# Redistributing eight levels' filler matmuls in a chunked gated recurrence: 2, 2, 3, 2, 2, 2, 1, 2 in place of two each

## The chip, the cores and the metric

One Trainium2 chip, one of its cores. The engines are TensorE (matrix products, PE in the profile), VectorE (DVE), ScalarE (ACT), GpSimd (POOL) and SyncE (SP, which here only issues transfers). The metric is the device time of the whole kernel in microseconds (us).

## The reference

The program is two residual blocks over 512 tokens of width 1024, in float32. The first block has two layers. In each, one large projection feeds three mixers: a gated recurrence with 8 heads (HGRN2), a latent attention with 8 heads, and a cross attention with 4 heads into a memory of 256 tokens. Their gated outputs are projected back, added and normalised. The second block has two feed-forward parts, a neighbourhood attention with a pooling branch, and a last gated part. The change touches only the recurrence:

```python
def _chunk_gated_recurrence(q, k, v, logf):
    """S_t = diag(f_t) S_{t-1} + k_t v_t^T ; o_t = S_t^T q_t, chunkwise."""
...
        decay = jnp.exp(jnp.minimum(diff, 0.0)) * tri[:, :, None]
        A = jnp.einsum('bhtsd,bhsd->bhts', qc[:, :, :, None, :] * decay, kc)
        o = (jnp.einsum('bhts,bhsv->bhtv', A, vc)
             + jnp.einsum('bhtd,bhdv->bhtv', qc * jnp.exp(b), state))
```

## The kernel before

The recurrence is computed in two groups of four heads per layer. A chunk is 128 tokens. Within a chunk the decayed scores are built in levels, doubling the distance that they span: level 0 is the diagonal, level 7 joins the two halves of 64. At level n, TensorE multiplies K blocks by Q blocks (L1094; 128 instructions at levels 0 to 5, 64 at levels 6 and 7) for four heads, into PSUM banks 4 to 7. VectorE then, in its phase of level n + 1, works in two pairs of heads: it takes the products of level n out of PSUM under a mask (L1923, from level 2 on), then multiplies a decay factor into Q (L1941), into K (L1942) and into the running factors (L1943). TensorE's level n waits for VectorE's pair 0 before head 0 and for pair 1 before head 2. So a level has two halves, and its second half is what can wait longer.

TensorE would be idle while VectorE works, so the function `beside` hands each level a number of pieces of a projection, which run behind the four heads' products. A projection of 1024 rows is a Block: two units of weights of 512 rows, four output banks (0 to 3), so eight pieces, each one unit on one bank. The order of pieces is fixed. In the first group it is: seven pieces of the values, eight of the gate, eight of the next group's queries. I write them by unit and bank: value pieces 01, 02, 03, 10, 11, 12, 13, gate pieces 00 to 13, query pieces 00 to 13. With two each, level 2 is followed by value pieces 11 and 12, level 3 by value piece 13 and gate piece 00, level 5 by gate pieces 03 and 10, level 6 by gate pieces 11 and 12.

A projection is computed in three passes (L902, L903, L904) from a high and a low part of each operand. For each tile of raw weights, loaded by SyncE (L832), ScalarE makes the high part (L1255) and GpSimd subtracts it from the raw tile to make the low part (L851). ScalarE does this two units ahead, and a unit's buffer is free only when TensorE has finished the unit three before it. So when a unit's last piece ends, the casts that waited for it follow at once, up to four, and GpSimd's subtractions behind them.

Finished banks are taken out by VectorE (values: a copy, L1631) or by ScalarE (gate: SiLU, L1276). VectorE reads them with a delay. It keeps a list of pending pieces: in each level, after the multiplications of pair 0, it takes pieces off until two are left, after those of pair 1 until one is left, and then adds the level's own pieces to the list.

After the levels come the turning of K (L1105), the states (L1112) and the read-out (L1118, L1120), each behind pieces of its own. The second group of a layer has its own call of `beside` with other blocks.

Of the kernel before, what the change touches and what calls it, by code (L numbers as in the profile page):

```python
# [121 lines left out]
def beside(blocks, *shares, first_pieces=()):  # L122


    pieces = list(first_pieces) + [pc for b in blocks for pc in b.pieces()]
    assert len(pieces) == sum(n for _, n in shares), (len(pieces), sum(n for _, n in shares))
    for ph, n in shares:
        first = 1 if len(ph.slots) > 1 and ph.kind != "level" else 0
        room = len(ph.slots) - first
        for i in range(n):  # L130
            ph.slots[first + i * room // n].append(pieces.pop(0))
# [171 lines left out]
def build(nc, x, x_t, mem_t, positions, w_in, w_uq, w_uk, w_uv, w_mk, w_mv, w_out, ln_g, ln_b, cols_in,  # L303
# [3 lines left out]
    with ctx:  # L307
# [47 lines left out]
        def col(name, i=0):  # L355
            return cols[:, COLS[name][0] + i:COLS[name][0] + i + 1]
# [68 lines left out]
        def transpose(src, tiles, dest, gain, src_fn=None):  # L425
            add(Phase("transpose", pe=tiles, act=tiles, dve=tiles, writes=dest, src=src, tiles=tiles,
                      dest=dest, gain=gain))
# [6 lines left out]
        def out_blocks(l, group):  # L434
            return [Block(w_cols(w_out[l], group * 512, 4, n * 512, 512), 4, 512, "nat", "z" if group == 3 else "y",
                          "residual_sum" if group == 3 else "residual", "dve", (n, group == 0)) for n in range(2)]
# [41 lines left out]
        for l in range(DEPTH):  # L478
            W = w_in[l]

            def blk(off, width, kind, evac, engine, arg, late=False):
                return Block(w_cols(W, 0, KD, off, width), KD, width, kind, "x", evac, engine, arg, late=late)
# [6 lines left out]
            for g in range(2):  # L489
                add(blk(HG_OFF[1] + 512 * g, 512, "tr", "forget", "act", None))  # L490
                add(Phase("forget", dve=1, layer=l, group=g))
                values = blk(HG_OFF[2] + 512 * g, 512, "nat", "copy", "dve", V)
                if g == 0:
                    add(queries[0])
                    add(Phase("between"))
                    plan[-1].slots[0] = values.pieces()[:1]
                else:
                    add(values)
                levels = [Phase("level", pe=4 if level <= LEVELS else 0, act=int(level in (3, LEVELS + 1)),
                                dve=0 if level == 0 else 4 + (level == LEVELS + 1), level=level, slots=2,  # L500
                                free_running=level > 0) for level in range(LEVELS + 2)]
                turn, states = Phase("key_turn", pe=3, act=3), Phase("states", pe=3, dve=3)
                read, gated = Phase("read_out", pe=4, act=4, dve=4), Phase("hg_norm", act=1, dve=1)
                gate = blk(HG_OFF[3] + 512 * g, 512, "nat", "silu", "act", G)
                ahead = latent if g else queries[1]
                if g == 0:

                    beside([gate, ahead], *((ph, 2) for ph in levels[:8]), (turn, 2), (states, 1), (read, 1), (gated, 3),
                           first_pieces=values.pieces()[1:])
                else:  # L510
                    beside([gate] + out_blocks(l, 0) + [ahead], *((ph, 2) for ph in levels[:8]), (turn, 2),
                           (states, 1), (read, 1), (gated, 4))
                for ph in levels:

                    ph.together = True
                for ph in levels + [turn, states, read, gated]:
                    add(ph)
                add(Late(ahead))
                transpose(G, 4, "y", col("hg_gain", l))
# [3 lines left out]
            gate = blk(MLA_GATE_OFF, 512, "tr", "silu", "act", G)  # L523
# [73 lines left out]
        def blk2(off, kind, evac, engine, arg, width=512, late=False):  # L597
            return Block(w_cols(w_in2, 0, KD, off, width), KD, width, kind, "x", evac, engine, arg,
                         banks=4 if kind == "nat" else width // P, late=late)
# [9 lines left out]
        gate, rest = blk2(2048, "nat", "sigmoid", "act", SG2), Phase("between")  # L609
# [1603 lines left out]
```

How the kernel before makes its waits and increments, by code:

```python
        def wait(eng, semaphore, value):  # L757
            if value > 0:
                eng.wait_ge(semaphore, value)
# [1 line left out]
        def units_over(eng, n):  # L761
            if n > 0:
                eng.wait_ge(*unit_end[n - 1])
# [46 lines left out]
        @block.sync  # L811
# [14 lines left out]
                if u == 10:  # L826
                    sp.dma_start(xs[:, :, :], x.rearrange("(t p) n -> p t n", p=P)).then_inc(x_loaded, 16)
                if u >= 2:
                    wait(sp, low_done, low_upto[u - 1][0])
                    wait(sp, low_done_dve, low_upto[u - 1][1])
                sp.dma_start(raw[:, u % 2, 0:nk, 0:b.width], b.w[:, k0:k0 + nk, :]).then_inc(raw_loaded[u % 2], 16)
            for t in range(T):
                for n in range(2):
                    sp.wait_ge(dve_step, finish.dve + 2 + 2 * t + n)
                    cut = slice(n * 512, (n + 1) * 512)
                    sp.dma_start(out[t * P:(t + 1) * P, cut], xs[:, t, cut]).then_inc(stored, 16)
            sp.wait_ge(stored, 16 * 2 * T)
# [2 lines left out]
        @block.gpsimd  # L842
        def _(pool):
            for u, (b, k0, nk) in enumerate(units):
                for k in range(nk):
                    if low_on_dve(u, k):
                        continue
                    pool.wait_ge(high_done, tiles_upto[u] + k + 1)
                    s = (slice(None), u % 3, k, slice(0, b.width))
                    pool.tensor_tensor(wl[s], raw[:, u % 2, k, 0:b.width], wh[s].bitcast(F32),
                                       ALU.subtract).then_inc(low_done, 1)
```

## Time and profile before

| | us |
|---|---|
| median of 3 runs | 2115.13 (2115.03 to 2115.35) |
| the profiled execution | 2115.07 |
| its span | 2113.3 |
| TensorE busy | 2089.2 (99%) |
| TensorE waiting for VectorE at the levels (L1094) | 2.6, in 2 waits |

The page gives each engine's busy time and its share of the span, and the span in 40 slices of about 53 us. The first groups of the two layers lie at 104 to 184 us and at 584 to 663 us. The view of stretches gives busy times between two times that are chosen, here the starts of two levels in sequence, so the length of a stretch is one level, its pieces and any wait.

### The profile page before, as it was taken

To read this page: it belongs to the slowest core of one execution; us is meant where nothing else is said; L and a number is where in the kernel's file an instruction comes from. 1 tells how busy PE (TensorE), PEld (TensorE's weight loads), DVE (VectorE), ACT (ScalarE), POOL (GpSimd) and SP (SyncE) were. 2 spreads that over 40 slices of the span, in tenths; PEclk is the share of its full clock that TensorE was granted. 3 is DMA by queue.
4 is the path that set the end of the run, shared out by engine and by line. 5 is a ranking of instruction groups with operands and counts; after the bars stand their busy time and mean duration, and the time that the engine had idled before them with its cause. 6 is when DMAs were issued, how large, how long until landed. Compare 5 with 4: busy or idle time off the path is not lost.

```text
span 2113.3 us, 33496 instructions
## 1 busy us (share of the span) xinstructions
PE 2089.2 (99%) x13820; PEld 1741.6 (82%) x13820; DVE 894.8 (42%) x1653; ACT 789.8 (37%) x1611; POOL 868.0 (41%) x680
## 2 busy tenths in 40 slices
PE   8999999999999999999999999999999999999998
PEld 7878888778978888778888888888888888888886
DVE  6173565535373465526432211433422612222264
ACT  5424335554423325455422222345433432222244
POOL 4633433232543433233354444343444345454423
PEclk9999999999999999999999999999999999999999
DMA  7522223122222223122242332242233133332222
GB/s 247 178 65 80 78 67 100 41 80 80 80 82 80 77 68 100 41 81 70 76 144 83 118 98 83 89 135 80 66 114 100 61 110 101 109 108 92 100 70 90
DMA packets 98679, 196.65 MB, mean 93 GB/s; under 512 B 3680, under 2 KB 12256, under 8 KB 98144
## 3 DMA queue, kind: packets, MB, share of 16 engines
q1 hardware_dynamic: 95072, 183.25, 26.6%
q10 hardware_dynamic: 3456, 11.27, 1.5%
q8 instruction: 109, 1.79, 0.3%
q14 instruction: 42, 0.34, 0.1%
HBM read 192.41 MB, written 2.10 MB: 92 GB/s over the span
## 4 chain that ended last, share of the span: by engine, by line
PE 59%; ACT 1%; DVE 0%; issue 0%; DVEq 0%
PE ps L902 18%; PE ps L903 18%; PE ps L904 18%; PE ps L1017 1%; PE ps L1157 1%; PE ps L1025 0%; PE ps L1034 0%; PE ps L1180 0%; PE ps L1200 0%; PE ps L1189 0%; PE ps L1070 0%; PE ps L1052 0%; ACT L1581 0%; PE ps L974 0%; PE ps L1210 0%; PE ps L1062 0%
## 5 line engine op out<-in xcount | busy, mean ns | idle before, releaser
L851 POOL TENSOR_TENSOR wl<-raw,wh 128x512 fp32r<-128x512 f32 (+2 forms) x676 | 867.8, 1307 | 1220.6 <-ACT wh L1255 1210.8
L1255 ACT CAST wh<-raw 128x512 fp32r<-128x512 f32 (+2 forms) x692 | 380.7, 604 | 773.3 <-PE ps L904 672.8
L902 PE MATMUL ps<-xh,wh 128*128 128x512 f32 (+1 forms) x1376 | 514.2, 374 | 1.2 <-issue 1.2
L904 PE MATMUL ps<-xh,wl 128*128 128x512 f32 (+1 forms) x1376 | 509.1, 370 | 0.0
L903 PE MATMUL ps<-xl,wh 128*128 128x512 f32 (+1 forms) x1376 | 508.7, 370 | 0.0
L902 PEld LDWEIGHTS ps<-xh,wh 128*128 128x128 f32 x1376 | 259.4, 189 | 46.1 <-issue 3.9
L904 PEld LDWEIGHTS ps<-xh,wl 128*128 128x128 f32 x1376 | 259.1, 188 | 44.6
L903 PEld LDWEIGHTS ps<-xl,wh 128*128 128x128 f32 x1376 | 259.4, 188 | 42.1
L902 PE MATMUL ps<-wh,xh 128*128 128x512 f32 (+1 forms) x608 | 239.1, 393 | 0.2 <-issue 0.2
L904 PE MATMUL ps<-wh,xl 128*128 128x512 f32 (+1 forms) x608 | 234.4, 386 | 0.0
L903 PE MATMUL ps<-wl,xh 128*128 128x512 f32 (+1 forms) x608 | 234.4, 385 | 0.0
L902 PE MATMUL ps<-wh,yh 128*128 128x512 f32 x496 | 198.0, 399 | 0.2
L904 PE MATMUL ps<-wh,yl 128*128 128x512 f32 x496 | 193.6, 390 | 0.0
L903 PE MATMUL ps<-wl,yh 128*128 128x512 f32 x496 | 193.4, 390 | 0.0
L1651 DVE TENSOR_TENSOR work<-ps,work 128x512 f32<-128x512 f32 x44 | 30.3, 688 | 383.3 <-PE ps L904 383.3
L902 PEld LDWEIGHTS ps<-wh,xh 128*128 128x128 f32 x608 | 114.2, 188 | 22.6 <-issue 1.4
L904 PEld LDWEIGHTS ps<-wh,xl 128*128 128x128 f32 x608 | 114.2, 188 | 21.8
L903 PEld LDWEIGHTS ps<-wl,xh 128*128 128x128 f32 x608 | 114.3, 188 | 20.4 <-issue 0.2
L902 PEld LDWEIGHTS ps<-wh,yh 128*128 128x128 f32 x496 | 93.3, 188 | 20.5 <-POOL wl L851 0.8
L904 PEld LDWEIGHTS ps<-wh,yl 128*128 128x128 f32 x496 | 93.1, 188 | 19.9
L903 PEld LDWEIGHTS ps<-wl,yh 128*128 128x128 f32 x496 | 93.3, 188 | 18.5
L1647 DVE TENSOR_TENSOR side<-side,ps 128x512 f32<-128x512 f32 x88 | 59.3, 686 | 106.0 <-PE ps L904 103.4
(273 smaller groups left out, 2436.2 us busy)
## 6 DMA issues: line engine op xcount, KB each, us to landing
raw<-w_in SPq DMA_DIRECT2D x58, 1024.0 KB, 5.2
raw<-w_out SPq DMA_DIRECT2D x20, 1024.0 KB, 5.0
raw<-f1g SPq DMA_DIRECT2D x10, 1024.0 KB, 5.1
raw<-f1u SPq DMA_DIRECT2D x10, 1024.0 KB, 5.1
raw<-f1d SPq DMA_DIRECT2D x10, 1024.0 KB, 5.0
raw<-f2g SPq DMA_DIRECT2D x10, 1024.0 KB, 5.2
raw<-f2u SPq DMA_DIRECT2D x10, 1024.0 KB, 5.1
raw<-f2d SPq DMA_DIRECT2D x10, 1024.0 KB, 5.1
```

The lines of the kernel that those rows point to most:

```text
L851: pool.tensor_tensor(wl[s], raw[:, u % 2, k, 0:b.width], wh[s].bitcast(F32), ALU.subtract).then_inc(low_done, 1)
L902: pe.matmul(o, still[0], move[0], start=k0 + k == 0, stop=False)
L903: pe.matmul(o, still[0], move[1], start=False, stop=False)
L904: mm = pe.matmul(o, still[1], move[0], start=False, stop=k0 + k == b.ktiles - 1)
L1017: mm = pe.matmul(ps[:, 4 + h, 0:width], q_heads[:, 2 * p + h, cut], k_heads[:, p, h, 0:width], start=True, stop=True)
L1157: mm = pe.transpose(ps[:, 4 + 2 * (t % 2) + b, f * P:(f + 1) * P], src[:, t, (4 * b + f) * P:(4 * b + f + 1) * P], ident[:, :])
L1255: act.copy(wh[:, v % 3, k, 0:width], raw[:, v % 2, k, 0:width]).then_inc(high_done, 1)
L1647: ins = dve.tensor_copy(dst, src) if first else dve.tensor_tensor(dst, dst, src, ALU.add)
L1651: link(dve.tensor_tensor(tmp, src, SG[:, j, :], ALU.mult))
```

## The change

The eight levels of the first group get 2, 2, 3, 2, 2, 2, 1 and 2 pieces. The total is 16 as before, and the order of the pieces is unchanged. A level with three pieces runs all three behind its four heads. Level 2 is now followed by value pieces 11, 12 and 13, level 3 by gate pieces 00 and 01, level 4 by 02 and 03, level 5 by 10 and 11, level 6 by 12 alone; level 7 keeps gate piece 13 and query piece 00.

```diff
                 if g == 0:
 
-                    beside([gate, ahead], *((ph, 2) for ph in levels[:8]), (turn, 2), (states, 1), (read, 1), (gated, 3),
+                    beside([gate, ahead], *((ph, n) for ph, n in zip(levels, (2, 2, 3, 2, 2, 2, 1, 2))), (turn, 2),
+                           (states, 1), (read, 1), (gated, 3),
                            first_pieces=values.pieces()[1:])
```

## Rows read from the trace of the kernel before

**Rows 1.** The page: engines' busy time; TensorE by slices.

```profile
PE 2089.2 (99%) x13820; PEld 1741.6 (82%) x13820; DVE 894.8 (42%) x1653; ACT 789.8 (37%) x1611; POOL 868.0 (41%) x680
PE   8999999999999999999999999999999999999998
```

**Rows 2.** Waits of TensorE, whole span: us in total, times, longest.

```profile
PE ps L1094 <- DVE work L1943: 2.6, 2, 1.3
```

**Rows 3.** Stretches, layer 0, levels 3, 4 and 6: length, engines' busy time (instructions), clock, DMA.

```profile
125.98:134.37 8.39, 7.09 (x154) 5.71 (x153) 8.18 (x15) 2.19 (x4) 1.86 (x2) 1.00 0.26 98
134.37:141.28 6.91, 6.91 (x154) 5.65 (x153) 6.58 (x10) 0.00 (x0) 4.11 (x3) 1.00 0.23 59
148.19:154.99 6.80, 6.80 (x89) 5.52 (x88) 4.43 (x8) 3.49 (x5) 2.58 (x2) 1.00 0.01 2
```

**Rows 4.** Stretches, layer 1, level 3.

```profile
605.50:613.90 8.40, 7.09 (x154) 5.71 (x153) 8.19 (x15) 2.19 (x4) 1.86 (x2) 1.00 0.27 102
```

**Rows 5.** Timeline of TensorE, level 3's second half, pieces, level 7: start, length.

```profile
128.02 0.73 PE L1094 MATMUL ps<-work 128*32 128x16 f32 x64 [1.30 <-DVE work L1943]
128.68 0.50 PE L902 MATMUL ps<-wh,xh 128*128 128x512 f32 x1
...
135.62 0.50 PE L902 MATMUL ps<-wh,xh 128*128 128x512 f32 x1
...
154.99 1.98 PE L1094 MATMUL ps<-work 128*32 128x64 f32 x64
```

**Rows 6.** Timeline of VectorE, its levels 3 to 5.

```profile
120.66 1.73 DVE L1941 TENSOR_TENSOR work<-work 128x512 f32<-128x512 f32 x1
122.32 1.77 DVE L1942 TENSOR_TENSOR work<-work 128x512 f32<-128x512 f32 x1
...
124.67 0.68 DVE L1631 COPY work<-ps 128x512 f32<-128x512 f32 x1
125.27 0.72 DVE L1923 COPY_PREDICATED work<-level_mask,ps 128x256 f32<-128x256 uint8 x1
...
127.35 0.61 DVE L1943 TENSOR_TENSOR work<-work 128x256 f32<-128x256 f32 x1
...
128.48 0.42 DVE L1923 COPY_PREDICATED work<-level_mask,ps 128x256 f32<-128x256 uint8 x1
...
130.26 0.44 DVE L1943 TENSOR_TENSOR work<-work 128x128 f32<-128x128 f32 x1
...
133.01 1.38 DVE L1943 TENSOR_TENSOR work<-work 128x128 f32<-128x128 f32 x1
...
135.18 0.43 DVE L1923 COPY_PREDICATED work<-level_mask,ps 128x256 f32<-128x256 uint8 x1 [0.19 <-PE ps L1094]
```

**Rows 7.** Timeline of VectorE, its level 7.

```profile
148.94 0.44 DVE L1923 COPY_PREDICATED work<-level_mask,ps 128x256 f32<-128x256 uint8 x1 [2.91 <-PE ps L1094]
149.41 0.69 DVE L1941 TENSOR_TENSOR work<-work 128x512 f32<-128x512 f32 x1
...
151.32 1.36 DVE L1941 TENSOR_TENSOR work<-work 128x512 f32<-128x512 f32 x1
...
153.32 0.19 DVE L1943 TENSOR_TENSOR work<-work 128x16 f32<-128x16 f32 x1
```

**Rows 8.** Timeline of GpSimd, the second burst and a single subtraction.

```profile
132.51 5.97 POOL L851 TENSOR_TENSOR wl<-raw,wh 128x512 fp32r<-128x512 f32 x4 [8.96 <-ACT wh L1255]
...
150.84 1.29 POOL L851 TENSOR_TENSOR wl<-raw,wh 128x512 fp32r<-128x512 f32 x1 [3.22 <-ACT wh L1255]
```

**Rows 9.** Timeline of ScalarE, casts of the second burst and the first SiLUs.

```profile
131.81 2.19 ACT L1255 CAST wh<-raw 128x512 fp32r<-128x512 f32 x4 [11.92 <-PE ps L904]
...
148.37 1.28 ACT L1276 ACT_TABLE_LOAD   x1 [2.11 <-PE ps L904]
149.66 0.60 ACT L1276 ACTIVATE work<-ps 128x512 f32<-128x512 f32 x1
...
152.38 0.60 ACT L1276 ACTIVATE work<-ps 128x512 f32<-128x512 f32 x1 [1.61 <-PE ps L904]
```

## The prediction

> **What bounds the kernel now.** I read the page first: TensorE is busy 99% of the span, and its row of slices shows nines from the second slice on [rows 1]. So a change can only count if it alters TensorE's work or its waits. The waits of TensorE come next [rows 2]: the matmuls of the recurrence's levels (L1094) waited for VectorE twice, 2.6 us in all, the only wait of the changed code. The table of stretches, one per level, shows where [rows 3, 4]: from one level's first matmul to the next it is 6.91 us for a level with two pieces, but 8.39 us after level 3 in layer 0 and 8.40 us after level 3 in layer 1. The chip spends 1.48 and 1.49 us there, 2.97 us in all. TensorE's rows show how it comes about [rows 5]: level 3 starts at 125.98 [rows 3] with heads 0 and 1, and its second half, heads 2 and 3, starts only at 128.02, 0.06 us after VectorE's L1943 (start 127.35, 0.61 long [rows 6]) ends. Level 3's second half needs what VectorE makes of level 2's second pair of heads.
>
> **What is removed.** A piece is 12 matmuls. Two SiLUs of ScalarE that follow pieces on their banks start 2.72 us apart (149.66 and 152.38) [rows 9], so a piece is 2.72 us of TensorE. With three pieces behind level 2, level 3 starts at 125.98 + 2.72 = 128.70. A level's half is 0.63 us (134.37 to the first piece behind it at 135.62 is 1.25 [rows 3, 5]), so its second half is due at 129.33. VectorE is a little later than before: level 3 of its program now finds four pieces pending and not three, so two bank copies (L1631) stand between its pairs of heads. One costs 0.60 (124.67 to 125.27 [rows 6]). Its pair ends at 127.96 + 0.60 = 128.56, 0.77 before it is needed. The wait goes: -1.48 us a layer.
>
> The total of pieces is 23 before and after, in the same order, with the same switches between levels and pieces. That costs nothing by itself. No DMA, matmul or copy is added. SyncE's loads follow GpSimd's subtractions and so move with them by up to 3 us; in the stretches concerned the DMA share is 0.01 to 0.26 and TensorE waits for no load [rows 3], so I cost that at nothing (uncovered, it would show as a wait of L902 for GpSimd). Bank reuse is free too: the first gate piece needs the copy that VectorE makes at 125.35, and starts near 130.
>
> **What is late next: level 4.** Here I think most of the gain goes. Moving a piece forward moves the end of its weight unit, and with it a burst of four high parts on ScalarE and four low parts on GpSimd. Before, that unit ended with the first piece behind level 3 (first matmul 128.68 [rows 5]), ScalarE's casts began 3.13 later at 131.81 [rows 9], and GpSimd's burst at 132.51, for 5.97 us [rows 8]. Now the unit ends with the third piece behind level 2: the burst comes 2.92 us earlier, from 129.59. VectorE's work for level 4 starts 0.81 after TensorE's level 3 (134.37 to 135.18 for the next level [rows 3, 6]), so at 129.51: the burst falls on the whole of it.
>
> What a GpSimd row does to a VectorE row with both inputs in SBUF is in the trace. L1941 at 151.32 took 1.36 and not the 0.69 of the one at 149.41; it ended 0.55 after the GpSimd row 150.84 + 1.29 [rows 7, 8]. Under the burst of level 2 two such rows took 1.73 and 1.77 [rows 6]. I read it as taking turns: VectorE waits for the GpSimd instruction to end, then does its own. Rows that read PSUM (L1923, L1631) keep their length.
>
> By turns, level 4 goes: L1923 at 129.51; L1941 waits for the first GpSimd instruction (to 130.88), ends 131.43; L1942 waits for the second (131.30 to 132.59), ends 133.14; L1943 waits for the third (133.00 to 134.29), ends 134.60; the fourth runs to 135.74 beside a bank copy and L1923, and the second pair is free of it. The same as a sum: before, this chain ran from 128.48 to 133.01 + 1.38 = 134.39, 5.91 us, with one held row in it (L1943, 1.38 for the 0.44 of the one at 130.26, so +0.94 [rows 6]). Bare it is 4.97. With three held rows, +0.78, +1.05 and +1.0, it ends at 129.51 + 4.97 + 2.83 = 137.3. TensorE's level 4 starts at 128.70 + 6.91 = 135.61 and wants its second half at 136.24. So it waits 1.1 us, and with the 0.06 of handing over and the 0.07 by which the old wait cost more than its gap (1.48 against 128.02 - 125.98 - 0.63 = 1.41) that is +1.2. Bounds: with no held row the chain ends at 134.5 and nothing is lost (0); with every one of the four turns taken from VectorE at 1.08 (1.77 less 0.69), it ends at 138.8, which is +2.7. I take 1.2, the turns as they fall.
>
> Level 5 is then free: its second half comes 1.2 later and the burst is over.
>
> **Level 7, which has one piece before it.** Level 6 to level 7 is 6.80 us now [rows 3]; with one piece it is 4.08. VectorE's work for level 7 started 0.75 after level 6 (148.19 to 148.94) and ended at 153.32 + 0.19, so 5.32 after it, of which 0.67 is the held L1941 [rows 7]; bare it ends at 4.65. TensorE wants the second half of level 7 at 4.08 + 0.95 = 5.03 (0.95 is half of level 7's 1.98 [rows 5], less the little by which its rows overlap what follows). Bare, there is 0.38 to spare; with one held row there is not. One is there: since the pieces behind level 5 are now gate pieces 10 and 11, the second of them ends 0.18 after level 6's start, as 10 did before (148.37 [rows 9]), and SiLU, cast and GpSimd's subtraction follow, the last 1.18 after the SiLU's start (149.66 to 150.84 [rows 8, 9]). GpSimd asks at 1.36 while L1941 of the first pair runs (1.22 to 1.91, from 149.41), takes its turn at 1.77 to 3.05, and L1942 ends at 3.60 and not 2.53: +1.07. The chain ends at 4.65 + 1.07 = 5.72, 0.69 late; with the same 0.13 it is +0.8. Bounds: 0 with no held row in time, and +1.5 with two.
>
> **The sum.** A layer: -1.48 + 1.2 + 0.8 = +0.5. Both layers show the same rows 479.5 us apart [rows 3, 4], so twice: +1.1 with the digits kept. The profiled execution took 2115.07 us (its span of 2113.3 and 1.8 around it), 0.06 below the median of the runs, 2115.13. Forecast: 2116.2 us, which is no change.
>
> The Trainium skill bears on this (SBUF — State Buffer, "Who interferes with whom"): a VectorE instruction with two SBUF inputs contends with a GpSimd instruction that reads SBUF, and whichever issues first keeps the shared ports for its whole length while the other is blocked. The rows above agree for the GpSimd row of 1.29 us [rows 7, 8]. Whoever left that rule out and took VectorE at its bare lengths would see no wait at levels 4 and 7 and come to 2115.07 - 2.97 = 2112.1, which is the second rival.
>
> **Rivals.**
> 1. Only level 4's wait appears, because GpSimd's subtraction at level 6 comes after L1942 or during a PSUM row: -1.48 + 1.2 = -0.3 a layer, 2114.5. For it: a margin of 0.38 before any held row. Against it: the request falls 0.4 us inside a row that shares. Its mirror, only level 7's wait (-0.7 a layer), gives 2113.7; for it speaks that VectorE's first row at level 4 starts near the burst and might win the first turn.
> 2. Neither appears and the whole wait is gained: 2112.1. For it, the bare lengths; against it, the held rows of [rows 6, 7] in the same loop.
> 3. Clearly slower: at level 4 each of the burst's four instructions takes a turn from VectorE, so the chain ends at 138.8 and the wait is 2.7. With level 7 as forecast: (-1.48 + 2.7 + 0.8) x 2 = +4.0, 2119.1. It is slower than before from the point where level 4 waits over 0.7. For it: two rows of 1.73 and 1.77 in sequence; against it: between the two pairs stand a bank copy and L1923, which pass beside the fourth.
>
> **How the numbers follow.** Forecast (both waits, sizes as above) 0.55; rival 1 with its mirror 0.25; rival 2 0.10; rival 3 0.06; something outside the group, of either sign, 0.04. The range 2112.8 to 2117.6 takes the forecast with sizes off by 0.7 us a layer and rival 1, and leaves out rival 2 and the far end of rival 3. A measurement of this kernel tells 0.2% (4.2 us) from no change; no case but rival 3's end and the unnamed one leaves that band, since even the whole wait is 0.14%. Faster 0.02, same 0.94, slower 0.04.
>
> **What would show it.** In the changed kernel's trace: level 3 in one piece, starting 2.7 us later, and 9.6 us from level 2 to level 3. GpSimd's second burst of the group near 129.6. The three rows of VectorE's first pair for level 4 at 1.4 to 1.8 us and a gap of 1.1 in L1094 ended by L1943. Level 6 to level 7 at 4.1 us, a gap of 0.7 in level 7. Level 7 of layer 0 starting near 154.7 where it was 154.99. I am wrong if level 4 shows no gap (the burst came elsewhere or takes no turns), or if a wait stands at another line, such as L902 for GpSimd.

## The result, and the profile after

The changed kernel took 2120.89 us (median of 10 runs, 2118.41 to 2121.64) against 2115.24 (10 runs, 2114.41 to 2117.65). The ratio is 1.0021, 95% interval 1.0012 to 1.0029. It is 0.2% slower, and the interval lies clear of 1, where no change was forecast and the range ended at 2117.6. The profiled execution took 2121.64, with a span of 2119.8.

Two parts of the trace hold 6.2 of the 6.5 us between the two spans. The first, with 1.44 and 1.42 us, is the group that was changed, once in each layer; the second, with 3.3 us, is the start of the program. The table of stretches gives, for the kernel before, both layers from the start of level 0 to the turning of K (start and end of the stretch, its length, then busy times):

```profile
104.56:167.92 63.36, 62.06 (x1114) 51.00 (x1114) 45.98 (x67) 15.03 (x24) 25.88 (x18) 1.00 0.24 78
584.09:647.45 63.36, 62.05 (x1113) 50.99 (x1113) 46.00 (x67) 15.02 (x24) 25.89 (x18) 1.00 0.24 79
```

And for the kernel after, the same two, and in layer 0 the stretches of levels 2, 3, 4, 6 and 7 (the last to its first piece):

```profile
107.90:172.70 64.80, 62.29 (x1114) 51.04 (x1113) 46.10 (x67) 14.93 (x24) 26.51 (x18) 1.00 0.23 76
...
588.94:653.72 64.78, 62.28 (x1114) 51.05 (x1114) 46.11 (x67) 14.93 (x24) 26.52 (x18) 1.00 0.24 77
...
123.66:132.04 8.38, 8.38 (x45) 6.68 (x37) 8.24 (x11) 0.00 (x0) 3.21 (x3) 1.00 0.39 127
132.04:138.99 6.95, 6.95 (x154) 5.66 (x153) 6.47 (x8) 2.19 (x4) 6.09 (x4) 1.00 0.01 2
138.99:147.00 8.01, 7.08 (x154) 5.71 (x153) 5.40 (x11) 0.00 (x0) 0.04 (x1) 1.00 0.42 133
...
153.92:158.00 4.08, 4.08 (x78) 3.27 (x77) 3.27 (x5) 1.10 (x2) 3.00 (x2) 1.00 0.01 4
158.00:161.68 3.68, 2.10 (x65) 1.85 (x64) 3.58 (x7) 1.10 (x2) 1.28 (x1) 1.00 0.03 3
```

The group grew by 1.44 and 1.42 us. Level 3 has lost its wait: 6.95 where it was 8.39 [rows 3]. (The stretch from 123.66 begins at the first of the three pieces behind level 2.) Level 4 now waits: 8.01 where 6.91 stood. Level 7, from its start to the first piece behind it, takes 3.68 where it took 1.91: before, it started at 154.99 [rows 5], and that piece at 156.90:

```profile
156.90 0.50 PE L902 MATMUL ps<-wh,xh 128*128 128x512 f32 x1
```

Per layer that is -1.44, +1.10 and +1.77. TensorE's waits after (us in total, times, longest) say the same. The first line is the start of the program, where one wait of 2.09 has been added; the second, for VectorE at the levels, was 2.6 in two waits [rows 2]:

```profile
PE ps L903 <- POOL wl L852: 10.7, 3, 8.0
PE ps L1095 <- DVE work L1944: 5.0, 4, 1.6
```

Lines are one higher than before, as the change adds one line of code. The timeline of TensorE, levels 4 and 7, shows both gaps before the second half:

```profile
138.99 0.74 PE L1095 MATMUL ps<-work 128*32 128x16 f32 x64
140.65 0.74 PE L1095 MATMUL ps<-work 128*32 128x16 f32 x64 [0.93 <-DVE work L1944]
...
158.00 1.09 PE L1095 MATMUL ps<-work 128*32 128x64 f32 x32
160.66 1.09 PE L1095 MATMUL ps<-work 128*32 128x64 f32 x32 [1.58 <-DVE work L1944]
```

VectorE's rows for level 4 (first pair and the copy behind it), then those that count of its chain for level 7:

```profile
132.85 0.44 DVE L1924 COPY_PREDICATED work<-level_mask,ps 128x256 f32<-128x256 uint8 x1 [0.37 <-PE ps L1095]
133.33 1.41 DVE L1942 TENSOR_TENSOR work<-work 128x512 f32<-128x512 f32 x1
134.67 1.78 DVE L1943 TENSOR_TENSOR work<-work 128x512 f32<-128x512 f32 x1
136.48 1.38 DVE L1944 TENSOR_TENSOR work<-work 128x128 f32<-128x128 f32 x1
137.78 0.67 DVE L1632 COPY work<-ps 128x512 f32<-128x512 f32 x1
...
155.76 1.79 DVE L1943 TENSOR_TENSOR work<-work 128x512 f32<-128x512 f32 x1
...
158.15 0.69 DVE L1942 TENSOR_TENSOR work<-work 128x512 f32<-128x512 f32 x1
158.76 0.68 DVE L1943 TENSOR_TENSOR work<-work 128x512 f32<-128x512 f32 x1
159.48 1.13 DVE L1944 TENSOR_TENSOR work<-work 128x16 f32<-128x16 f32 x1
```

And what GpSimd did in the same time:

```profile
132.90 6.13 POOL L852 TENSOR_TENSOR wl<-raw,wh 128x512 fp32r<-128x512 f32 x4 [6.03 <-ACT wh L1256]
...
153.85 3.15 POOL L852 TENSOR_TENSOR wl<-raw,wh 128x512 fp32r<-128x512 f32 x2 [4.70 <-ACT wh L1256]
159.29 1.28 POOL L852 TENSOR_TENSOR wl<-raw,wh 128x512 fp32r<-128x512 f32 x1 [2.29 <-ACT wh L1256]
```

I call a VectorE row held when it takes longer than the same row does alone because a GpSimd instruction runs. At level 4 three rows are held, one by each of the first three subtractions. At level 7 two are: L1943 at 155.76 by the second of a pair, and L1944 at 159.48, a row of 0.19 that ends 0.04 after the subtraction 159.29 + 1.28. That subtraction follows the SiLU of gate piece 12, the one piece behind level 6:

```profile
158.11 0.60 ACT L1277 ACTIVATE work<-ps 128x512 f32<-128x512 f32 x1 [2.98 <-PE ps L905]
```

Before, the subtraction behind the first of the two pieces of level 6 came 0.05 after VectorE's last row had ended (153.32 + 0.19 [rows 7]):

```profile
153.56 1.29 POOL L851 TENSOR_TENSOR wl<-raw,wh 128x512 fp32r<-128x512 f32 x1 [1.43 <-ACT wh L1255]
```

The second part is the start of the program, which the change does not touch. Level 0 began at 107.90 and not at 104.56, 3.3 us later. TensorE's timeline after has a wait there, and behind it a low clock. First the matmul that waited:

```profile
48.32 0.47 PE L903 MATMUL ps<-wh,yh 128*128 128x512 f32 x1 [2.09 <-POOL wl L852]
```

The same matmul before:

```profile
46.46 0.47 PE L902 MATMUL ps<-wh,yh 128*128 128x512 f32 x1
```

It starts 1.9 us later; the other 1.5 of the 3.3 us are lost behind it. Then the stretches 46 to 50 and 50 to 54 us of the kernel after, by the table of stretches (TensorE's granted clock is the third number from the end):

```profile
46.00:50.00 4.00, 1.91 (x9) 1.15 (x8) 4.00 (x3) 4.00 (x9) 3.79 (x3) 0.96 0.00 2
50.00:54.00 4.00, 4.00 (x12) 3.19 (x12) 4.00 (x8) 1.66 (x2) 3.26 (x2) 0.61 0.59 167
```

The same stretches before:

```profile
46.00:50.00 4.00, 3.92 (x18) 2.83 (x17) 4.00 (x5) 3.77 (x6) 4.00 (x4) 1.00 0.12 13
50.00:54.00 4.00, 4.00 (x19) 3.30 (x18) 4.00 (x6) 0.28 (x1) 1.43 (x1) 1.00 0.89 281
```

TensorE worked 1.91 of 4 us and then, for a while, at 1.2 and not 2.4 GHz (the mean granted clock of 50 to 54 us is 0.61): 12 matmuls in 50 to 54 where 19 stood.

### The profile page after: what moved, and what is told of

The parts are those of the page before. It is cut to its first block, busy times and chain, and to the rows that moved or that the text cites. A ratio compares the mean times of both kernels' runs of the same rounds, so it can differ in the third digit from the quotient of the medians.

```text
span 2119.8 us, 33496 instructions
## 1 busy us (share of the span) xinstructions
PE 2090.9 (99%) x13820; PEld 1742.8 (82%) x13820; DVE 894.9 (42%) x1653; ACT 789.8 (37%) x1611; POOL 869.2 (41%) x680
## 4 chain that ended last, share of the span: by engine, by line
PE 58%; ACT 1%; DVE 0%; DMA 0%; issue 0%; DVEq 0%; ACTq 0%
PE ps L903 18%; PE ps L904 18%; PE ps L905 18%; PE ps L1018 1%; PE ps L1158 1%; PE ps L1026 0%; PE ps L1035 0%; PE ps L1181 0%; PE ps L1201 0%; PE ps L1190 0%; PE ps L1071 0%; PE ps L1053 0%; ACT L1582 0%; DMA work<-post_gains 0%; DMA work<-p_t 0%
```

## The experiments

### The changed kernel again

The same file. A late start means here a run some 3 us above the lowest of its kernel, as the profiled run above was.

> The changed kernel once more. In its profile the group lost 1.44 us a layer (2.9 in all) and 3.3 us stood ahead of it, in the first 60 us: weights landed 1.8 us later, TensorE waited 2.1 us at 48 us and then ran 3.4 us at half clock. Theory A: the start of the program lands in one of two ways whatever the change, so the change itself costs 2.9 us; with many runs of both kernels each shows some with the late start, and runs at a mean clock of 1.000 differ by 2.9 (2118.1 against 2115.2). Theory B: the change makes the late start more frequent, and its medians stay 5 to 6 us above the kernel before.

Measured: 2118.54 (11 runs, 2117.65 to 2121.01) against 2115.41 (33 runs, 2114.48 to 2118.16); ratio 1.0015, interval 1.0006 to 1.0024. The group took 64.78 in the profile; the start this time had a wait of 0.49 and no low clock, and level 0 began at 104.15. The lowest runs differ by 3.2. Of the runs of the kernel before, 13 of 33 lie above 2116, so its times scatter in the same way. That speaks for theory A: the medians differ by 3.1 and not by 5 to 6. The condition on the mean clock did not sort the runs: the one at 2117.65 shows 0.999.

### One piece behind level 7 and two behind level 6

```diff
-zip(levels, (2, 2, 3, 2, 2, 2, 1, 2))
+zip(levels, (2, 2, 3, 2, 2, 2, 2, 1))
```

> 2, 2, 3, 2, 2, 2, 2, 1: the piece is taken from behind level 7 and not from behind level 6. Theory A (the wait at level 7 comes from the short filler behind level 6 plus VectorE rows held by GpSimd): the gap of 1.58 in level 7 is gone, the one of 0.92 in level 4 stays, and the turning of K, which had some 5 us to spare, shows no new wait. Group: 63.36 - 1.48 + 1.10 = 63.0 us from level 0 to the turning, against 64.80 in the changed kernel; total 0.8 below the kernel before, starts being equal. Rival: the wait is moved to the turning of K (L1106), and the group stays at 64.8.

Measured: 2114.87 (2114.10 to 2117.22), ratio 0.9999, interval 0.9990 to 1.0008. Its stretches of level 4, of level 6 to 7, of level 7 to the turning of K, and the whole group:

```profile
135.73:143.73 8.00, 7.07 (x153) 5.71 (x152) 5.40 (x11) 0.00 (x0) 0.04 (x1) 1.00 0.42 133
150.65:157.45 6.80, 6.80 (x90) 5.52 (x89) 5.82 (x8) 2.21 (x4) 4.29 (x3) 1.00 0.01 2
157.45:167.65 10.20, 10.20 (x101) 8.63 (x101) 6.59 (x11) 4.24 (x6) 4.28 (x3) 1.00 0.33 104
104.65:167.65 63.00, 62.07 (x1113) 50.98 (x1113) 48.26 (x67) 14.93 (x24) 26.96 (x18) 1.00 0.24 79
```

63.00, as worked out. TensorE is busy throughout the two last levels: the wait at level 7 is gone and none has come at the turning. Level 4 keeps its own. The group is 0.36 us shorter than before (63.00 against 63.36), so the loss of the change hangs on where the missing piece was taken from. The median is 0.5 below the kernel before, where 0.8 was expected, and the interval holds 1.

### GpSimd's subtractions made short

```diff
+            queries[1].short = True
...
+                    if b.short:
+                        s = (slice(None), u % 3, k, slice(0, 8))
-                    pool.tensor_tensor(wl[s], raw[:, u % 2, k, 0:b.width], wh[s].bitcast(F32),
+                    pool.tensor_tensor(wl[s], raw[:, u % 2, k, s[3]], wh[s].bitcast(F32),
```

> The changed kernel, but GpSimd's low parts of the next group's queries (the burst on level 4 and the ones on level 7) are made for 8 of 512 columns only, so that each instruction is short; the rest of those low parts is left as it was. Theory: VectorE's rows there are held by GpSimd's, so they fall back to 0.69, 0.69 and 0.44, both gaps (0.92 in level 4, 1.58 in level 7) vanish, and the group takes 63.36 - 1.48 = 61.9 us; total 5.8 below the changed kernel. Rival: the gaps come from the later start of VectorE's work and the extra bank copy in it; then they stay within 0.2 us and the time too.

Measured: 2112.52 (2112.03 to 2115.02), ratio 0.9985, interval 0.9977 to 0.9994; the group took 61.90 and TensorE has no wait at the levels. The median is 6.0 below the changed kernel's, where 5.8 was expected. VectorE's first pair at level 4, and the four short subtractions beside it:

```profile
129.88 0.69 DVE L1946 TENSOR_TENSOR work<-work 128x512 f32<-128x512 f32 x1
130.49 0.69 DVE L1947 TENSOR_TENSOR work<-work 128x512 f32<-128x512 f32 x1
131.22 0.46 DVE L1948 TENSOR_TENSOR work<-work 128x128 f32<-128x128 f32 x1
```

```profile
129.46 0.21 POOL L856 TENSOR_TENSOR wl<-raw,wh 128x8 fp32r<-128x8 f32 x1 [6.02 <-ACT wh L1260]
129.98 1.43 POOL L856 TENSOR_TENSOR wl<-raw,wh 128x8 fp32r<-128x8 f32 x3 [0.31 <-ACT wh L1260]
```

No other instruction was altered. So both waits come from the length of GpSimd's instructions; the later start of VectorE's work and the extra bank copy alone make none. The time is that of the forecast's second rival (2112.1), but only with GpSimd out of the way.

### The load of x later

```diff
-                if u == 3:
-                    sp.dma_start(x_raw, x_t).then_inc(xt_loaded, 16)
...
+                if u == 4:
+                    sp.dma_start(x_raw, x_t).then_inc(xt_loaded, 16)
```

(the new place is behind the load of the unit, the old one ahead of it)

> The changed kernel, but the load of the transposed x (2 MB), which is issued ahead of the fourth unit of weights, is issued behind the fifth. Theory A on the start: the fourth unit no longer shares with it and lands early, TensorE waits nowhere between 10 and 60 us and keeps its clock: all runs near 2118.2 or below, at a mean clock of 1.000, none at 2120 or above. Rival: the late start comes from something else (the order of engines, the clock by itself), and runs at 2120.4 to 2121.6 stay as frequent as in the changed kernel; or the fifth unit is now late and TensorE waits for it.

Measured: 2119.82 (2117.50 to 2120.30), ratio 1.0015, interval 1.0006 to 1.0024. A miss: 7 of 11 runs lie above 2119. The profiled run is the fastest of the eleven, so it doesn't show what the slower ones had, but ScalarE's rows show how the wait can stay: the fourth unit came at 21.44 and not at 25.88, but the sixth, whose load now stands behind that of x, came only at 33.30, after ScalarE had waited 4.93 for it, and TensorE still waited 1.36 near 46 us.

```profile
21.44 2.18 ACT L1256 CAST wh<-raw 128x512 fp32r<-128x512 f32 x4 [3.16 <-DMA raw<-w_mv]
...
33.30 2.18 ACT L1256 CAST wh<-raw 128x512 fp32r<-128x512 f32 x4 [4.93 <-DMA raw<-w_mk]
39.71 1.28 ACT L1332 ACT_TABLE_LOAD   x1 [4.22 <-DVE work L1744]
```

The last row points on: ScalarE then idles 4.22 us for VectorE's angles, with the casts that TensorE wants next queued behind them.

### The start altered: the seventh unit ahead of the angles

```diff
                 elif e.kind == "angles":
+                    high(6)
+                    ahead[:] = 7, 0
                     act.wait_ge(dve_step, e.dve + 1)
...
                     dve.memset(rope_table[64:128, 1, :], MLA_SCALE)
+                    low(6, 1)
+                    low(6, 3)
...
-                if u >= 8:
+                if u >= 8 or u == 6:
                     return
```

On the kernel before:

> The kernel before (two pieces each), with the start altered only: ScalarE casts the seventh unit of weights ahead of its wait for the rotary angles, and VectorE's two low parts of that unit stand ahead of the angles' last step. Theory on the start: TensorE's wait for GpSimd near 46 us (0.3 to 2.1 us in the profiles so far) is late because those casts stand behind a chain that begins with a load landing at 24 or at 26 us, and a long wait there is followed by 3.4 us at half clock. Without it the runs are close together: median 2114.3 (0.3 to 0.7 below the lowest runs of the kernel before are possible), none above 2116. Rival (the clock or the load is what scatters, not this wait): as many runs between 2116 and 2118 as in the kernel before, 14 of 33.

On the changed kernel:

> The changed kernel (2, 2, 3, 2, 2, 2, 1, 2) with the same altered start. If the change costs only what the group shows, this is 2 x 1.44 = 2.9 us above the kernel before with the same start, median to median (near 2117.2). If the change also acts on the start, the difference is 5 us or more, as it was between the two kernels in the first measurement (5.65).

Measured: 2114.18 (2113.55 to 2114.89) and 2117.05 (2116.44 to 2119.17), against 2116.46 for the kernel before (32 runs, 2114.67 to 2118.09, 17 of them above 2116); ratios 0.9987 (0.9978 to 0.9996) and 1.0004 (0.9995 to 1.0013). (The 14 of 33 in the expectation is 13 by the list of runs.) With the start altered the two kernels differ by 2.87 us, twice the 1.44 of the group, and their runs do not overlap. The first one's stretches 46 to 50 and 50 to 54 us have a full TensorE at a full clock:

```profile
46.00:50.00 4.00, 4.00 (x19) 3.31 (x18) 3.91 (x7) 4.00 (x7) 4.00 (x3) 1.00 0.55 212
50.00:54.00 4.00, 4.00 (x20) 3.30 (x19) 4.00 (x3) 1.04 (x3) 4.00 (x3) 1.00 0.67 203
```

So the change costs 2.9 us. Without the wait near 46 us the runs of the kernel before spread over 1.3 us and none lies above 2116, where 17 of 32 did: this wait, with what follows it, is what scatters. One run of the changed kernel (2119.17) is still 1.65 above the next, and no run shows why.

### Three behind levels 2 and 3, none behind level 7

```diff
-zip(levels, (2, 2, 3, 2, 2, 2, 1, 2))
+zip(levels, (2, 2, 3, 3, 2, 2, 2, 0))
```

The start as it was:

> 2, 2, 3, 3, 2, 2, 2, 0, the start as it was: a third piece behind level 3 gives VectorE's held work for level 4 another 2.7 us, level 7 has no piece, and the two in front of the turning of K are all that cover VectorE's last phase (7.5 us wanted there, 6.3 to 7.5 needed). Worked out from the turns of the ports: no wait at levels 3, 4 and 7, group 63.36 - 1.48 = 61.9 us, total 3.0 below the kernel before (near 2112). Rival: the turning of K now waits, up to 1 us a layer, and the total is 1 to 2 below.

With the altered start:

> 2, 2, 3, 3, 2, 2, 2, 0 with the altered start: the two add up, as they lie 50 us apart. Median 3.0 below the kernel before with the altered start, near 2111.3, and runs within 1 us of each other. Rival: the wait at the turning of K (1 to 2 us in all) takes a part, or the start scatters as before.

Measured: 2112.20 (2111.46 to 2114.53), ratio 0.9982 (0.9973 to 0.9991), and 2111.76 (10 runs, 2111.12 to 2112.41), ratio 0.9978 (0.9969 to 0.9987). The first one's stretches of level 3, of level 6 to 7, of level 7 to the turning of K, and the group:

```profile
128.54:138.20 9.66, 9.66 (x165) 7.90 (x164) 8.07 (x10) 2.19 (x4) 6.11 (x4) 1.00 0.15 40
152.04:158.84 6.80, 6.80 (x89) 5.52 (x88) 5.84 (x8) 2.26 (x5) 3.09 (x2) 1.00 0.37 118
158.84:166.33 7.49, 7.49 (x89) 6.37 (x89) 5.87 (x11) 3.18 (x4) 2.83 (x2) 1.00 0.09 35
104.39:166.33 61.94, 61.94 (x1113) 50.91 (x1113) 47.58 (x67) 15.03 (x24) 26.84 (x18) 1.00 0.24 80
```

TensorE is busy for the whole of the group. GpSimd's burst (6.11 us) still falls on VectorE's level 4, where the third piece now hides it, and the two pieces before the turning cover VectorE's last phase. Both versions are faster than both kernels, than the kernel before by 0.2%. The altered start with the new distribution gave a median 2.42 lower than the altered start alone, where 3.0 was expected, and runs within 1.3 us of each other.

## Why the prediction was wrong

**The wait at level 3** was to go, and went: -1.44 (6.95 against 8.39) where -1.48 was said.

**Level 4** was to wait 1.2 and waits 1.10. The chain started 0.81 after level 3, as worked out, and its held rows took 1.41, 1.78 and 1.38, so 2.75 us more than bare, where 2.83 was said. The turns of the two engines were right, and the run with short subtractions shows that GpSimd is the cause: the rows of the same chain took 0.69, 0.69 and 0.46 there. The Trainium skill (SBUF — State Buffer, "Who interferes with whom") says that a VectorE instruction with two SBUF inputs contends with a GpSimd instruction that reads SBUF, and calls the ports that they share an exclusive lock. The trace agrees: each of the first three subtractions held one row.

**Level 7** is the step that failed, in size. The sentence "with one held row there is not. One is there" counted the subtraction behind gate piece 11 and stopped. The one behind piece 12 comes too: piece 12 is now the only one behind level 6, ends after 4.19 us (SiLU at 158.11), and 1.18 later, at 159.29, GpSimd asks, 0.19 before VectorE's last row. That row took 1.13 for 0.19. The end of the chain for which 5.72 was given came at 160.61 - 153.92 = 6.69, the gap was 1.58 and not 0.7, and the term +1.77 and not +0.8. The prediction's bound, two rows and +1.5, had no chance of its own and was 0.3 too low. The second hold could have been worked out from the prediction's rows: the first piece behind level 6 has its SiLU at 152.38 [rows 9], 4.19 after level 6's start at 148.19 [rows 3]; with the 1.18 GpSimd asks at 5.37, and the last row was to start at 5.72 - 0.19 = 5.53. Before, that subtraction had missed the chain by 0.05; the first held row moved the chain's end into its way.

**The sum** for the group was therefore +1.1 where the group gives +2.9. From 2115.07, where the forecast began, that is 2117.9, 0.3 beyond the range: the group alone is enough to leave it.

**The start** was not in the sum. The three runs of before lay within 0.32 us and I took this for the scatter. With 65 more runs the kernel before spreads over 3.7 us, 30 of them above 2116. With the wait of TensorE near 46 us removed, most of that spread is gone. Six profiles have the start as it was. In five of them the fourth unit landed at 23.9 to 24.2 us and this wait is at most 0.7 us; in the sixth, the late one, it landed at 25.9, the wait is 2.09 us, and the clock fell behind it. No second late run was profiled, so that the others are late in the same way is likely and not shown. The first comparison had more late starts on the side of the changed kernel: 8 of its 10 runs lie above 2120 and 3 of the 10 before above 2116, while of the repeated ones it was 3 of 11 and 13 of 33. With the start altered the kernels differ by 2.87, so the other 2.8 of the 5.65 us came in by the start and not by what the change does in the group. Why the landing scatters is open.

**Rivals.** Rival 3 (2119.1) had the right sign and the wrong place: it put the extra at level 4, so that it lies nearest to what was measured is luck. Rival 1, only level 4's wait, is what two pieces behind level 6 gave: 0.36 a layer gained where 0.3 was said. Rival 2, the whole wait gained, needed a third piece behind level 3 and none behind level 7.

## What to carry to other kernels

When filler is moved between waits of a chain, list every instruction of the other engines that moves with it, the last one included, and lay each against the chain's rows; the wait that is removed may be due to the same bursts, and they move too (two rows of VectorE's work for level 3 took 1.73 and 1.77 under one [rows 6]). Take filler from a place whose follower has slack to the end of its chain (here in front of the turning of K, where 5 us were to spare), not from one where 0.4 us were. A wait of TensorE that is near zero in the profile can be the largest scatter of the kernel: look at its distribution, or remove it, before a change of 0.1% is judged.

## What the runs showed of the hardware

A VectorE row with both inputs in SBUF that meets a running GpSimd subtraction ends only behind it: a row of 0.69 us alone ended 0.55 after the subtraction, one of 0.19 ended 0.04 after it and took 1.13, so a small row can lose as much as a large one. In a burst the two engines alternate, one instruction each, and both lose: four subtractions that take 1.28 or 1.29 alone took 6.13 together at level 4. A copy out of PSUM beside the fourth of them kept its 0.67.

In one profile, after a wait of 2.09 us, TensorE's granted clock averaged 0.61 over 50 to 54 us; waits of 0.49 and 1.36 were followed by 1.00 in two other profiles.
